# Another load order for the expert weights, one second matrix loaded early into a spare stretch, one gate bias row instead of two

## The reference

```python
# mixture of experts, 32 experts, D = 1024, D_EXPERT = 512
y_e = (silu(x_e @ w1[e]) * (x_e @ w3[e])) @ w2[e]     # x_e: the tokens routed to e
x = x + sum(gate_weight * y_e)                        # two experts per token

def hybrid_layer(x, ctx, c, c_ctx, w_mod, b_mod, ...):
    shift, scale, gate = adaln_params(c, w_mod, b_mod)            # c @ w_mod + b_mod, cut in three
    shift_c, scale_c, gate_c = adaln_params(c_ctx, w_mod, b_mod)  # the same b_mod
    ...
    x = x + gate[:, None, :] * y
    if with_ctx_out:
        ctx = ctx + gate_c * yc
```

## Time and profile before

| | us |
|---|---|
| median of 3 runs | 1792.14 |
| lowest and highest | 1791.32, 1792.4 |
| the profiled execution, its own time | 1790.95 |
| its span, first to last instruction | 1789.2 |
| PE busy | 1738.2 (97%) |
| PEld busy | 960.2 (54%) |
| DVE busy | 740.0 (41%) |
| ACT busy | 551.2 (31%) |
| DMA moved | 324.07 MB, mean 181 GB/s |

### The profile page before, as it was taken

One profiled execution on the slowest core, in us unless ns is written; L12 is line 12 of the kernel. 1 busy time (PEld: TensorE's weight loads), 2 busy tenths in 40 slices (PEclk: granted clock), 3 DMA queues, 4 the chain that ended last, 5 costly groups with the idle time before them and its releaser, 6 DMA issues. The chain is left out here.

```text
span 1789.2 us, 24625 instructions
## 1 busy us (share of the span) xinstructions
PE 1738.2 (97%) x9806; PEld 960.2 (54%) x9806; DVE 740.0 (41%) x1583; ACT 551.2 (31%) x1121; POOL 152.5 (9%) x192
## 2 busy tenths in 40 slices
PE   8999988999999999999899999999999999999998
PEld 4433466455555445555464444677645544566663
DVE  2244477142512122333134125577524328466642
ACT  2111487223101112343124212455412233444420
POOL 0310000001111111111100014000000002000000
PEclk9999999999999999999999999999999999999999
DMA  8665598379999999999871131000201012000001
GB/s 285 234 221 188 89 87 237 134 285 402 417 414 415 416 416 418 417 418 418 355 285 39 55 119 70 1 2 1 107 3 36 24 44 91 25 1 2 9 17 47
DMA packets 93057, 324.07 MB, mean 181 GB/s; under 512 B 13048, under 2 KB 29432, under 8 KB 67856
## 3 DMA queue, kind: packets, MB, share of 16 engines
q1 hardware_dynamic: 79088, 302.02, 46.0%
q10 hardware_dynamic: 8656, 12.07, 1.9%
q0 software_dynamic: 5200, 8.41, 1.3%
HBM read 316.53 MB, written 14.06 MB: 185 GB/s over the span
## 5 line engine op out<-in xcount | busy, mean ns | idle before, releaser
L2305 PE MATMUL tail_ps<-arena 128*128 128x512 f32 x488 | 213.4, 593 | 1.1 <-DMA arena<-in_w_plg 1.1
L1200 PE MATMUL mix_ps<-arena 128*64 128x256 f32 x1568 | 180.0, 382 | 3.4 <-DVE arena L1750 1.8
L1071 PE MATMUL mix_ps<-arena,side 128*128 128x512 f32 x384 | 171.1, 603 | 0.7 <-DMA arena<-in_w_in 0.7
L507 DVE TENSOR_SCALAR_CACHE_REDUCE arena<-tail_ps 128x768 f32<-128x768 f32 x128 | 117.5, 956 | 114.1 <-PE tail_ps L365 69.8
L2305 PEld LDWEIGHTS tail_ps<-arena 128*128 128x128 f32 x488 | 91.8, 190 | 111.6 <-issue 111.1
L1200 PEld LDWEIGHTS mix_ps<-arena 128*64 128x64 f32 x1568 | 110.2, 137 | 70.7 <-issue 18.8
L1212 PE MATMUL mix_ps<-arena 128*64 128x512 f32 x512 | 119.7, 610 | 11.7 <-DMA arena<-in_w 8.4
L1071 PEld LDWEIGHTS mix_ps<-arena,side 128*128 128x128 f32 x384 | 72.7, 193 | 96.9 <-issue 95.0
L2305 PE MATMUL tail_ps<-arena,side 128*128 128x512 f32 (+2 forms) x328 | 123.6, 535 | 0.0
L595 ACT ACTIVATE arena<-arena,tail_small 128x768 f32<-128x768 f32 x128 | 118.1, 926 | 6.4 <-DVE arena L507 6.4
L384 PE MATMUL tail_ps<-first,arena 128*128 128x128 f32 x768 | 97.8, 277 | 0.5 <-ACT arena L595 0.5
(11 more groups left out here) (418 smaller groups left out, 2420.8 us busy)
## 6 DMA issues: line engine op xcount, KB each, us to landing
arena<-in_w SPq DMA_DIRECT2D x81, 2048.0 KB, 24.9
arena<-in_l_w_mod SPq DMA_DIRECT2D x16, 1024.0 KB, 5.9
arena<-in_l_w_in SPq DMA_DIRECT2D x16, 1024.0 KB, 6.9
sixth<-in_w SPq DMA_DIRECT2D x15, 1024.0 KB, 19.0
sixth<-in_w SPq DMA_DIRECT2D x15, 896.0 KB, 21.5
arena<-in_w_in SPq DMA_DIRECT2D x12, 1024.0 KB, 9.3
arena<-in_l_w_mod SPq DMA_DIRECT2D x16, 512.0 KB, 6.5
arena<-in_l_w_in ACTq DMA_DIRECT2D x12, 512.0 KB, 10.9
```

What stands on the lines that cost most here:

```text
L507: dve.tensor_scalar(self.rows_of(n, x), self.scores_of(n, x), -1.0, None, ALU.mult, ALU.min, accum_out=nm[:, b, x:x + 1]).then_inc(s["maxe ...
L1071: last = pe.matmul(ps[:, u % 4], oT[:, k, t * P:(t + 1) * P], weights.slot(W_IN[n, k // 4], 4, 512)[:, k % 4], start=(k == 0), stop=(k == ...
L1200: last = pe.matmul(out[h * CAP:(h + 1) * CAP, 0:H2], x, block_of(k, h), start=(k == 0), stop=(k == DK - 1))
L2305: last = pe.matmul(out, lhs(k), rhs(k), start=(k == 0), stop=(k == K - 1))
```

## The change

Four things change. The order of the ring becomes second, first, third (`w2[e-1], w1[e], w3[e]`), with `w3[2]` before it in the place that `w2[0]` had. `w2[0]` leaves the ring: it is loaded in two pieces into the stretch of `base` that will later hold the second block's tables and layer 0's gate, when the near attention is done. `w1[0]` is issued later, with `w1[1]`, and `w3[1]` earlier, with `w3[0]`. Of the gate biases of layer 0 one row is loaded instead of two, after the product with `w2[0]`, and `add_gate` writes both conditions from it; so the gate rows are spread in iterations 2 to 4 instead of 1 to 3, and the first context tile is turned in iteration 5 instead of 4.

```diff
-    matrix_at = [view(proj_w, 0, 4096), view(proj_w, 4096, 4096), view(ring, SLOT, 4096), view(ring, 3 * SLOT, 4096), view(proj_w, 8192, 4096), None]
-    once, ONCE = view(work, 4096, 4096), ("w2", 1)
-    asked = [("w1", 0), ("w3", 0), ("w1", 1), ("w3", 1), ("w2", 0), ("w1", 2), ("w3", 2)]
+    matrix_at = [view(ring, 3 * SLOT, 4096), view(proj_w, 4096, 4096), view(ring, SLOT, 4096), view(proj_w, 0, 4096), view(proj_w, 8192, 4096), None]
+    SPARE = 2592
+    spare = base[:, XT * D + CT * D:XT * D + CT * D + 2 * SPARE].rearrange("p (a w) -> p a w", w=SPARE)[:, :, 0:2 * D]
+    once = {("w2", 0): spare, ("w2", 1): view(work, 4096, 2, 2 * D)}
+    asked = [("w1", 0), ("w3", 0), ("w1", 1), ("w3", 1), ("w3", 2), ("w1", 2)]
     for e in range(3, STATIC + 1):
-        asked += [("w1", e), ("w3", e), ("w2", e - 1)]
+        asked += [("w2", e - 1), ("w1", e), ("w3", e)]
...
+    def blocks_once(v):
+        return lambda f, h: v[:, f // 2, f % 2 * D + h * 512:f % 2 * D + (h + 1) * 512]
+    second_blocks = lambda e: blocks_once(once["w2", e]) if ("w2", e) in once else blocks_out(matrix_at[use_of("w2", e) % PLACES])
...
             sp.wait_ge(s["near_pv"], near.N)
-            expert(0, "w1")
             expert(0, "w3")
+            expert(1, "w3")
+            expert(0, "w2")
...
-            for gate, conds, src in gate_of:
-                for x in conds:
-                    sp.dma_start(gate[:, x], src).then_inc(s["gates_in"], 16)
+            def gates_in(gate, conds, src):
+                sp.dma_start(gate[:, conds[0]], src).then_inc(s["gates_in"], 16)
+            gates_in(*gate_of[1])
             sp.wait_ge(s["out_mm"], 8)
+            expert(0, "w1")
             expert(1, "w1")
-            expert(1, "w3")
...
-            expert(0, "w2")
-            for e in range(2, STATIC):
-                if e > 2:
-                    expert(e, "w1")
-                expert(e, "w3")
-                if e == 2:
-                    continue
-                expert(e - 1, "w2")
-                if e == 4:
+            expert(2, "w3")
+            for which, e in asked[PLACES:]:
+                if e < STATIC:
+                    expert(e, which)
+                if (which, e) == ("w1", 4):
+                    sp.wait_ge(*used("w2", 0))
+                    gates_in(*gate_of[0])
+                if (which, e) == ("w3", 4):
                     sp.wait_ge(*used("w2", 1))
                     sp.dma_start(side_gain, A["g_ple"]).then_inc(s["side_gain"], 16)
-            expert(STATIC - 1, "w2")
...
                 if e in range(1, 4):
                     turn_mods(e - 1)
-                    spread_gate(2 * e - 2)
-                    spread_gate(2 * e - 1)
-                if e in (4, 6):
-                    t = (e - 4) // 2
+                if e in range(2, 5):
+                    spread_gate(2 * e - 4)
+                    spread_gate(2 * e - 3)
+                if e in (5, 6):
+                    t = e - 5
...
             def add_gate(n):
-                gate = mods[0][2][:, n // 2] if n < 4 else mods[1][2][:, 0]
-                to = gate[:, n % 2 * 512:(n % 2 + 1) * 512]
-                dve.wait_ge(s["gates_in"], 48)
+                gate = mods[0][2] if n < 4 else mods[1][2]
+                half = slice(n % 2 * 512, (n % 2 + 1) * 512)
+                dve.wait_ge(s["gates_in"], 32)
                 dve.wait_ge(s["mod_spread"], n + 1)
-                dve.tensor_tensor(to, to, ps[:, 6 + n % 2], ALU.add).then_inc(s["mod_added"], 1)
+                dve.tensor_tensor(gate[:, 1 if n < 2 else 0, half], gate[:, 0, half], ps[:, 6 + n % 2], ALU.add).then_inc(s["mod_added"], 1)
```

More of the change, by code:

```diff
@@ L795, in first_layer @@
     used = lambda which, e: (s[dict(w1="h1", w3="h3", w2="y")[which]], e + 1)
-    matrix_in = lambda which, e: (s["once_in"], 16) if (which, e) == ONCE else (s["w"][use_of(which, e) % PLACES], (48 if split(which, e) else 16) * (use_of(which, e) // PLACES + 1))
+    matrix_in = lambda which, e: (s["once_in"], 16 * len(once)) if (which, e) in once else (s["w"][use_of(which, e) % PLACES], (48 if split(which, e) else 16) * (use_of(which, e) // PLACES + 1))
     wide_in = lambda v: v.rearrange("p (k n) -> p k n", n=D_EXPERT)
@@ L810, in first_layer, with blocks_out @@
     first_blocks = lambda which, e: blocks_sixth if split(which, e) else blocks_in(matrix_at[use_of(which, e) % PLACES])
-    second_matrix = lambda e: wide_out(once if ("w2", e) == ONCE else matrix_at[use_of("w2", e) % PLACES])
+    def blocks_out(v):
+        return lambda f, h: wide_out(v)[:, f, h * 512:(h + 1) * 512]
+    def blocks_once(v):
+        return lambda f, h: v[:, f // 2, f % 2 * D + h * 512:f % 2 * D + (h + 1) * 512]
+    second_blocks = lambda e: blocks_once(once["w2", e]) if ("w2", e) in once else blocks_out(matrix_at[use_of("w2", e) % PLACES])
     late_at = dict(w1=(matrix_at[1], used("w1", STATIC - 2)), w3=(matrix_at[2], used("w3", STATIC - 2)), w2=(matrix_at[4], used("w1", STATIC - 1)))
-    assert [use_of(*k) % PLACES for k in (("w1", STATIC - 2), ("w3", STATIC - 2), ("w1", STATIC - 1), ("w2", STATIC - 2))] == [1, 2, 4, 0]
+    assert [use_of(*k) % PLACES for k in (("w1", STATIC - 2), ("w3", STATIC - 2), ("w1", STATIC - 1), ("w2", STATIC - 2))] == [1, 2, 4, 3]
     weights = Weights([view(ring, i * SLOT, SLOT) for i in range(SLOTS - 1)] + [view(work, 6144, SLOT)], s["loaded"])
@@ L965, in expert @@
             def expert(e, which):
-                if (which, e) == ONCE:
-                    sp.dma_start(runs(once), A[which][e].rearrange("(a p j) n -> p a (j n)", a=2, p=P)).then_inc(s["once_in"], 16)
+                if (which, e) in once:
+                    sp.dma_start(once[which, e], A[which][e].rearrange("(a p j) n -> p a (j n)", a=2, p=P)).then_inc(s["once_in"], 16)
                     return
@@ L1206, in turn_hidden, with second_product @@
                 return last
-            def second_product(wb):
+            def second_product(block_of):
                 for f in range(FK):
@@ L1211, in second_product @@
                     for h in range(2):
-                        last = pe.matmul(py[h * CAP:(h + 1) * CAP, :], x, wb[:, f, h * 512:(h + 1) * 512], start=(f == 0), stop=(f == FK - 1))
+                        last = pe.matmul(py[h * CAP:(h + 1) * CAP, :], x, block_of(f, h), start=(f == 0), stop=(f == FK - 1))
                 return last
@@ L1902, in _ @@
                     take_mods(e - 1)
-                    add_gate(2 * e - 2)
-                    add_gate(2 * e - 1)
+                if e in range(2, 5):
+                    add_gate(2 * e - 4)
+                    add_gate(2 * e - 3)
                 if e == 3:
```

6 lines of the change are left out of this document (3 added, 3 removed).

## The result

| | median of runs | lowest to highest |
|---|---|---|
| before | 1791.81 us (4 runs) | 1791.32 to 1792.4 |
| after | 1801.98 us (4 runs) | 1800.2 to 1802.82 |

The ratio is 1.0056, with a 95% interval of 1.0044 to 1.0068: the change makes the kernel slower, by about 10 us. The profiled execution of the changed kernel took 1800.2 us, its span 1798.4 us (before: 1789.2).

The account below looks back on a forecast made before the run. The prediction took the DMA stream of the expert loop, from 398 us to its end, as the bound. Net lag 5.0 plus third gap 3.5 gave +8.5 us, from the median 1800.6 us; 8-in-10 range 1793 to 1806.5.

Parts of the forecast that it names:

- First gap: Early expert loop: `w1[4]` waits for `h3` of iteration 2 until 423.0 us, the queue empty for 2.6 us.
- Second gap: Next round: `w2[4]` waits for `y` of iteration 3 until 441.6 us, the queue done at about 438 to 440.
- Fixed point: Set `w2[4]`, `w1[5]`, `w3[5]` complete: stream 3.5 to 5.8 us late there, 5.0 taken, net of byte saving and both gaps.
- The -3.8 us of bytes: Full DMA stretch of the expert loop: net 1.573 MB less at 0.416 MB/us saves 3.8 us.
- Rival 1: Expert loop's loads: the order costs nothing and the bytes alone count, 1788.3 us; chance 0.10.
- Context tile: VectorE, iteration 5: first tile ahead of side tiles makes TensorE go on at 487.4 us, 5.5 later, standing still 8.7.
- no gap in the next two rounds: Two rounds after the fixed point: loads issued before the queue runs dry, ending near 476 and 493 us.
- if the wait on VectorE is shorter than 6 us: TensorE before the product of iteration 6: sign by which the forecast falls; 8 to 9 us idle would show it right.
- Third gap: About 494 us: loads waiting for `y` of iteration 6's product leave DMAs idle 0.6 to 3.3 us; 3.5 taken.
- Afterwards: Later rounds: 4.5 us left in the queue, DMAs stay full, the lag is passed on to the gate products.
- Rival 3: Loop from 690 to 866 us: late gaps of 1 to 3 us per round bring +14, 1806 us; chance 0.14.
- Rival 2: Start of the loop: saving and gaps cancel through slack at 398 to 418 us, +1.5, 1793.6 us; chance 0.14.

Follow-up runs that it names:

- e3: Changed kernel with ring order back to first, third, second and the first context tile's VectorE gain moved to iteration 6; 1790.23 us.
- e6: e3 with TensorE's and VectorE's small work of iterations 1 to 4 moved one iteration back; 1787.56 us.
- e4: Changed kernel with `w2[0]` loaded as late as before, ahead of `w3[2]`, still into its two idle pieces; 1801.31 us.
- e1: Changed kernel with only the ring's order set back to first, third, second; 1790.93 us.
- e2: Changed kernel, order as changed, with the first context tile's VectorE gain moved from iteration 5 to 6; 1797.88 us.
- e8: Changed kernel, order as changed, with the first context tile turned and gained in iteration 4 again; 1796.99 us.
- e7: e3 with the changed order (second, first, third) from the round of expert 8 on; 1790.79 us.
- e5: e3 with `w2[0]` loaded late again, ahead of `w3[2]`; 1791.27 us.
- e9: e3 with the changed order (second, first, third) only in the rounds of experts 3 to 5; 1796.48 us.
- e10: e6 with `w2[0]` loaded late again, ahead of `w3[2]`; 1790.83 us.

## Why the prediction was right

*Bound.* It rested on the DMA stream of 398 to 890 us setting the end. That held in the main: with the 8.6 us of loop time lost (512.4 - 503.8) come three windows in which the DMA share falls, and both go together (e3: 10.6 back). It needed two limits. Before 444 us the stream is bound by the places that TensorE frees as much as by bytes (e3, e6). And near the end TensorE is as tight as the stream: before, it waits four times for loaded weights from 866 us on (3.5 us in all) and 1.28 us more ahead of the gate products; in the changed kernel its trace puts no wait down to a load from 690 us on, and at the gate products the last load lands at 901.4 us and TensorE comes free at 901.5. The lag is 9.2 us at 515 us and 8.8 at the gate products. The rate was 411 to 418 GB/s again. The Trainium skill (DMA: Bandwidth & Descriptors, Where 436 GB/s comes from) lets about 358 GB/s bind for loads from HBM. The Trainium skill (Perfetto Trace Analysis, Engine Utilization) says that a core whose neighbour is idle can pull up to about 435; this case's windows, 411 to 418, agree with the second.

*First gap.* Given as issue at 423.0, landing at 430.5 to 432.2; measured 423.44 and 431.9. *Second gap.* Issue 441.6, landing 449.1 to 450.8; measured 441.91 and 450.0. The bounds from the earlier trace rows held the lone load both times, and nearly the third time (9.6 us). The Trainium skill's fit for one DMA (DMA: Bandwidth & Descriptors, Anatomy of one DMA: 2.0 us and the bytes over 436 GB/s, measured there for the GpSimd path) would give an estimate of 6.8 us; the trace shows 8.1 to 9.6. *Fixed point.* 459.1 to 461.4 for the set that was done at 455.6; measured 461.6, so +6.0 where 5.0 was taken, and just outside the 3.5 to 5.8 given. This term was mis-sized by 1.0 us: the two loads behind the lone one took 11.6 us, not 10.0 to 10.6. The DMAs moved 424 GB/s in these 11.6 us, 4.9 MB, of which the two matrices are 4.2; the prediction had left too little room for the other transfers.

*The -3.8 us of bytes.* Not a term of its own in the sum, and rightly: e4 shows that the gaps swallow nearly all of it. Rival 1 (the bytes alone count, 1788.3) has its condition in e6, not here.

*Context tile.* TensorE was to go on at 487.4; it did at 487.70. Its idle time was to be 8.7 us in one piece and was 5.67, because 1.41 and 1.23 us of waits for `w1[6]` and `w3[6]` came before it. The step "no gap in the next two rounds" didn't foresee these: 6 us late, the stream reached TensorE's needs already in iteration 6. They cost nothing, since VectorE set the end of that stretch; without them (e1) the wait is 8.45 us. By its own sign ("if the wait on VectorE is shorter than 6 us") the forecast should have fallen here, and 8 to 9 us of idle time was one of the things that would show it right. The sign was badly chosen: what counts is when TensorE goes on, and that came as forecast. The product ran partly at the lower of the two clock levels (granted clock 0.55 in 484 to 490 us) and took 5.49 us, not 6.40, so `y` came at 493.2, between the 491.1 and 493.8 given. The nine waits of up to 1.3 us don't contradict what the prediction cites on the clock: that section of the Trainium skill (TensorE: Matmul & The Clock Gate, HAM oscillation) tells of longer waits. *Third gap.* Taken 3.5 us. Before, the round that ends with `w2[6]` was done at 488.1 and after at 494.1 (+5.9); one round later it is 505.6 and 514.8, +9.2: there the gap is worth 3.3 us. At the end of the loop it is less: taking it away brings 2.2 us of loop time in e2 and 2.8 in e8. That 3.5 was so near is in part luck: the product was 0.9 us shorter than the 6.40 taken, and the lone load behind it 2.1 us longer than the 7.5.

*Afterwards.* The DMAs stayed full in all late rounds, 1.02 and 1.01 from 600 to 866 us, and e7 puts a price of at most 0.7 us on the order there. Rival 3 (late gaps) is so refuted; from 690 to 866 us 411 GB/s moved instead of 416 at the same share. That goes with the order in the late rounds (411 to 413 in e2, e4, e7 and e8, 415 to 417 in e1, e3, e5, e6, e9 and e10) and is not explained; e7's 0.7 us of loop time is the price that was measured.

*Sum.* 6.0 + 3.3 is 9.3 at 515 us, and it is 8.8 at the gate products, +8.5 foreseen. One term was 1.0 us too small and the other too large, so the sum is nearer than its parts. The medians differ by 10.2, the spans of the two traces by 9.2; where the last 1.0 us comes from isn't shown. The forecast of 1800.6 us was 1.4 us low. Rival 2 (saving and gaps cancel) fell with the sizes of the gaps: nothing of them was won back by slack at 398 to 418, where the share was already 0.98 before and after.

## What to carry over

An in-order queue of prefetches is only as deep as its first waiting entry: put the load whose place comes free last at the end of its round, not at its head, and look first at the rounds in which the queue is short: here nearly all of the cost arose there. To know whether taking bytes out of a full stretch will pay, add up the DMA time at rest at its start, which told the worth here to 1 or 2 us: there the places are the bound, and moving 2.5 us of small work behind the products that free them (e6) let 3.4 of the 3.8 us of saved bytes through, where 2.0 had come before. Two stalls priced one by one don't add when the same queue bridges both.

## What the runs showed of the hardware

The granted clock answers to one and the same short wait in two ways. Ahead of the first product of the tail TensorE waits 2.53 to 2.56 us in all twelve traces. Before, and in e2, e5, e6 and e8, the product behind it takes 3.69 us; in the changed kernel (its line is shown above) and the six others 5.15 to 5.38 us. Before, e6 and e3:

```profile
909.20 3.69 PE L2305 MATMUL tail_ps<-extra,arena 128*128 128x256 f32 x16 [2.53 <-PEq L164]
```

```profile
905.95 3.69 PE L2314 MATMUL tail_ps<-extra,arena 128*128 128x256 f32 x16 [2.56 <-PEq L164]
```

```profile
908.12 5.38 PE L2316 MATMUL tail_ps<-extra,arena 128*128 128x256 f32 x16 [2.53 <-PEq L164]
```

The same holds in iteration 6, where e3 and e6 both wait 2.07 us at 482.06 us and the product takes 5.29 us in the one and 3.65 in the other:

```profile
482.06 5.29 PE L1222 MATMUL mix_ps<-arena 128*64 128x512 f32 x16 [2.07 <-issue]
```

```profile
482.06 3.65 PE L1222 MATMUL mix_ps<-arena 128*64 128x512 f32 x16 [2.07 <-issue]
```

From 600 to 690 us the changed kernel has waits of 1.3 to 1.6 us and a clock of 1.00; behind those of 3.24, 5.67 and 8.45 us the product was long each time. So a wait of 2 to 2.6 us costs the product behind it 0 or 1.5 to 1.7 us here. The kernel loses less of it: from the gate products' start to the end the changed kernel's trace is only 0.4 us longer than that of the kernel before, with a product longer by 1.7. One such fall lowers the mean clock by about 1.7/1785, 0.001 (an estimate); the runs of e6 lie between 0.995 and 0.999, so it seems to vary between executions of one kernel too. What decides it no run here shows. It accounts for little of the scatter that can be seen: e6's runs at 0.998 or 0.999 have a median of 1787.3 us, the others 1787.8. The runs of one kernel spread over 1 to 4 us, so a difference under about 1 us between two medians says little by itself, and the loop time stands beside it.
